# RWKV-7 scan in one backbone layer: one score product per head over four PSUM banks, growth on the transposed matrix, and a new order of steps

## What is computed

```
def step(s, inp):
    w_t, k_t, v_t, kk_t, a_t = inp[:5]
    sa = jnp.einsum('bhvk,bhk->bhv', s, kk_t)
    s = (s * w_t[:, :, None, :] - sa[..., None] * (kk_t * a_t)[:, :, None, :]
         + v_t[..., None] * k_t[:, :, None, :])
    if not want_out:
        return s, None
    return s, jnp.einsum('bhvk,bhk->bhv', s, inp[5])
```

## Time and profile before

| | |
|---|---|
| median of 3 runs | 2215.66 us (2215.59 to 2217.02) |
| the profiled execution | 2217.15 us, of which its span is 2215.5 us |
| busy TensorE, VectorE, ScalarE | 2059.9, 1346.1, 811.3 us |
| mean granted TensorE clock | 0.963 of full |
| the scan | from about 971 us to 1256 us of the span |

### The profile page before, as it was taken

One profiled execution on the slowest core, in us unless ns is written; L12 is line 12 of the kernel. 1 busy time (PEld: TensorE's weight loads), 2 busy tenths in 40 slices (PEclk: granted clock), 3 DMA queues, 4 the chain that ended last, 5 costly groups with the idle time before them and its releaser, 6 DMA issues. The chain is left out here.

```text
span 2215.5 us, 37507 instructions
## 1 busy us (share of the span) xinstructions
PE 2059.9 (93%) x16171; PEld 1695.2 (77%) x16171; DVE 1346.1 (61%) x1258; ACT 811.3 (37%) x890; POOL 278.1 (13%) x135
## 2 busy tenths in 40 slices
PE   7679999999899989977889899979999999999998
PEld 3258888888678876656788788868888888888886
DVE  3465666665628637767888577365665656554444
ACT  1232212123063225625555455354343434333333
POOL 0242213123103305401000020000000000000000
PEclk9589999999989999989999899999999999999999
DMA  9988898987173449996544377535555555555553
GB/s 328 349 284 324 308 322 287 325 309 220 48 219 86 108 139 270 313 236 174 108 89 84 53 223 272 200 123 190 187 188 186 188 188 189 189 193 200 196 189 114
DMA packets 406658, 454.09 MB, mean 205 GB/s; under 512 B 108062, under 2 KB 357262, under 8 KB 389246
## 3 DMA queue, kind: packets, MB, share of 16 engines
q1 hardware_dynamic: 398912, 441.04, 62.9%
q10 hardware_dynamic: 7614, 11.10, 1.4%
HBM read 413.89 MB, written 38.22 MB: 204 GB/s over the span
## 5 line engine op out<-in xcount | busy, mean ns | idle before, releaser
L215 DVE TENSOR_TENSOR f_w_lo<-t_w_raw,f_w_hi 128x2048 fp32r<-128x2048 f32 x132 | 302.3, 2290 | 306.8 <-ACT f_w_hi L209 306.8
L270 PE MATMUL pf<-h,f_w_hi 128*128 128x512 f32 x1320 | 463.9, 395 | 0.0
L209 ACT ACTIVATE f_w_hi<-t_w_raw 128x2048 fp32r<-128x2048 f32 x132 | 253.2, 1918 | 445.6 <-PE pf L270 283.6
L269 PE MATMUL pf<-h,f_w_lo 128*128 128x256 f32 x1320 | 367.4, 278 | 0.3 <-DVE h L2666 0.3
L270 PEld LDWEIGHTS pf<-h,f_w_hi 128*128 128x128 f32 x1320 | 247.6, 188 | 54.3
L269 PEld LDWEIGHTS pf<-h,f_w_lo 128*128 128x128 f32 x1320 | 248.3, 188 | 4.6 <-DVE h L2666 0.6
L209 ACT ACTIVATE p_w_hi<-h_w_raw 128x2048 fp32r<-128x2048 f32 (+1 forms) x52 | 96.4, 1901 | 340.4 <-DVE stage L726 252.1
L261 PE MATMUL p_in<-h,p_w_lo 128*128 128x512 f32 (+1 forms) x512 | 199.3, 389 | 0.0
L259 PE MATMUL p_in<-h,p_w_hi 128*128 128x512 f32 (+1 forms) x512 | 199.3, 389 | 0.0
L260 PE MATMUL p_in<-h,p_w_hi 128*128 128x512 f32 (+1 forms) x512 | 199.2, 389 | 0.0
L858 DVE SCALAR_TENSOR_TENSOR late_acc<-h_of_x,siluc,late_acc 128x2048 f32<-128x2048 f32 x60 | 160.9, 2682 | 38.0 <-DMA h_of_x<-in_ada_w 36.5
(11 more groups left out here) (408 smaller groups left out, 3352.8 us busy)
## 6 DMA issues: line engine op xcount, KB each, us to landing
h_of_x<-in_ada_w SPq DMA_DIRECT2D x64, 1024.0 KB, 5.0
h_w_raw<-in_w_in SPq DMA_DIRECT2D x51, 1024.0 KB, 7.4
t_w_raw<-in_ffn_w_gate SPq DMA_DIRECT2D x44, 1024.0 KB, 5.1
t_w_raw<-in_ffn_w_up SPq DMA_DIRECT2D x44, 1024.0 KB, 5.1
t_w_raw<-in_ffn_w_down SPq DMA_DIRECT2D x44, 1024.0 KB, 4.9
h_w_raw<-in_ada_w SPq DMA_DIRECT2D x32, 1024.0 KB, 8.8
gate_w<-in_w_in SPq DMA_DIRECT2D x32, 1024.0 KB, 6.1
t_w_raw<-in_w_out SPq DMA_DIRECT2D x16, 1024.0 KB, 5.9
```

The costliest lines, as they stand in the source:

```text
L209: act.activation(self.hi[:, m % self.S, 0:w], self.raw[:, s, 0:w], ACT.Copy)\
L215: eng.tensor_tensor(self.lo[:, m % self.S, 0:w], self.raw[:, s, 0:w], b32(self.hi[:, m % self.S, 0:w]), ALU.subtract)\
L269: pe.matmul(hi, wl, x[:, 0, k, :], start=False, stop=False)
L270: return pe.matmul(both, wh, x[:, :, k, :], start=False, stop=last)
```

## The change

`pa` and `pb` become two halves of one tile `pab` of four banks. `scores1` is now the only product of scores. For a latent half chunk the stationary operand is both sources of a head (128 columns) and the moving one both queries (128 columns), so that all four blocks of scores of a head come from one product; for a context half chunk only the query kk moves (64 columns). `first` is twice as wide and holds what `first` and `t2` held. `scores2`, `scores3` on TensorE, `scores2` on VectorE and `t2` are gone. Because the sources are stationary now, the matrix arrives transposed; growth goes on with it transposed (masks of the other direction, operands of `inverse` swapped). The transpose in `open_` is two instructions of 64 partitions each. Every `run_...` list is in another order; `prepare` of VectorE and the exponential after it stand one turn of the loop earlier.

```
-        first = pair_of("first", [U8, C])
+        first = pair_of("first", [2 * U8, C])
-        t2 = pair_of("t2", [U8, C])
-        pa = [psum(st, f"pa{d}", 2 * U8 * C) for d in range(2)]
-        pb = [psum(st, f"pb{d}", 2 * U8 * C) for d in range(2)]
+        pab = [psum(st, f"pab{d}", 4 * U8 * C) for d in range(2)]
+        pa = [p[:, 0:2 * U8 * C] for p in pab]
+        pb = [p[:, 2 * U8 * C:4 * U8 * C] for p in pab]
+        def scored(c, d, q):
+            if not latent(c):
+                return whole(pb[d])
+            return pab[d][:].rearrange("p (n q c) -> p n q c", q=2, c=C)[:, :, q, :]
...
                 def turn(c, d, l, src):
-                    dve.transpose(turned[d][:], src).then_inc(sm("turned", d), 1)
+                    for rows, at in src:
+                        dve.transpose(quads(turned[d][:])[rows], at).then_inc(sm("turned", d), 1)
...
                 def scores1(c, d):
...
-                    dve.copy_predicated(quads(first[d][:]), mask(LOWER, d).bitcast(mybir.dt.uint32), narrow(pb[d]))\
+                    dve.copy_predicated(first[d][:], every_head(STRICT, d).bitcast(mybir.dt.uint32), scored(c, d, 0))\
                        .then_inc(sm("first", d), 1)
-
-                def scores2(c, d):
-                    dve.wait_ge(sm("t2s", d), c + 1)
-                    dve.tensor_tensor(quads(t2[d][:]), narrow(pa[d]), mask(STRICT, d), ALU.mult).then_inc(sm("t2", d), 1)
...
+                    if latent(c):
+                        pe.wait_ge(sm("q2", d), c - 3)
                         pe.wait_ge(sm("S", d), c)
                     for j, h in UNITS:
-                        last = pe.matmul(by_other(pa[d], j, h), source(s12[d], j, h, 1), feat(q12[d][:, :, 0, :], j, h),
-                                         start=True, stop=True)
-                    last.then_inc(sm("t2s", d), 1)
...
+                        sources = s12[d][HEAD[h], j].rearrange("p a c -> p (a c)")
+                        if latent(c):
+                            at = block_of(j, h) * 2 * C
+                            last = pe.matmul(pab[d][:, at:at + 2 * C], sources, q12[d][HEAD[h], j].rearrange("p q c -> p (q c)"),
+                                             start=True, stop=True)
+                        else:
+                            last = pe.matmul(by_block(pb[d], j, h), sources, feat(q12[d][:, :, 0, :], j, h), start=True, stop=True)
...
                 def run_vector(step):
...
-                        every("prepare", 0)
...
+                        every("open", 1)
+                        every("prepare1", 0)
+                        context("stage", 1, 1)
+                        latents("prepare2", 0)
+                        latents("stage", 1, 1)
+                        context("prepare2", 0)
+                        context("stage", 1, 2)
+                        every("prepare", -1)
+                        latents("stage", 1, 2)
```

More of the change, by code:

```diff
@@ L1411, in _ @@
                     dve.tensor_copy(eyes_r[HEAD[h]], own.unsqueeze(1).broadcast_to([C, U8 // 2, C])).then_inc(sm("init", 0), 1)
-                    for t in cross + first:
+                    for t in cross:
                         dve.tensor_copy(t[HEAD[h]], own.unsqueeze(1).broadcast_to([C, U8, C])).then_inc(sm("init", 0), 1)
@@ L1417, in _ @@
                     dve.memset(e2[d][:, :, edge:edge + 1], math.exp(REF)).then_inc(sm("init", 0), 1)
+                dve.wait_ge(sm("cleared", 0), 2)
+                for t in first:
+                    for h in range(2):
+                        own = eye[HEAD[h], HEAD[h]]
+                        dve.tensor_copy(own_blocks(t, h)[HEAD[h]].rearrange("p h u c -> p u h c"),
+                                        own.unsqueeze(1).unsqueeze(1).broadcast_to([C, U8 // 2, 2, C])).then_inc(sm("init", 0), 1)
                 dve.wait_ge(sm("init", 0), 17)
-                dve.wait_ge(sm("cleared", 0), 2)
+                dve.wait_ge(sm("cleared", 0), 4)
                 def prepare(c, d):
@@ L1459, in stage @@
                     dve.wait_ge(sm("level", d), c * GROW + l)
-                    turn(c, d, l, narrow(level(d, l - 1)))
+                    turn(c, d, l, [(slice(0, P), narrow(level(d, l - 1)))])
                 def scores1(c, d):
@@ L1494, in open_ @@
                         dve.wait_ge(sm("step", d), c * GROW)
-                    turn(c, d, 0, first[d][:])
+                    turn(c, d, 0, [(HEAD[b], own_blocks(first[d], b)[HEAD[b]]) for b in range(2)])
                 def state(c, d):
@@ L1637, in _ @@
             def _(pool):
-                for t in S:
+                for t in first + S:
                     pool.memset(t[:], 0.0).then_inc(sm("cleared", 0), 1)
@@ L1649, in _ @@
                 pe.wait_ge(sm("init", 0), 17)
-                pe.wait_ge(sm("cleared", 0), 2)
+                pe.wait_ge(sm("cleared", 0), 4)
                 FOURS = [[(j, 0), (j + 1, 1), (j, 1), (j + 1, 0)] for j in range(0, U8, 2)]
@@ L1718, in flips @@
                 def flips(c, d):
-                    pe.wait_ge(sm("t2", d), c + 1)
+                    pe.wait_ge(sm("first", d), c + 1)
+                    if latent(c):
+                        pe.wait_ge(sm("r12", d), c - 3)
+                    elif c:
+                        pe.wait_ge(sm("S", d), c)
                     for j in range(U8):
@@ L1733, in grow @@
                         pe.wait_ge(sm("vt", d), 2 * c + 2)
-                    src, of = (grown, held(l - 1)) if l else (first, tok)
+                    of = held(l - 1) if l else tok
                     for j, h in UNITS:
-                        last = pe.matmul(placed(l)(level(d, l), j, h), of(step[d], j, h), of(src[d], j, h),
+                        grows = of(grown[d], j, h) if l else first[d][HEAD[j % 2], block_of(j, h), :]
+                        last = pe.matmul(placed(l)(level(d, l), j, h), of(step[d], j, h), grows,
                                          start=True, stop=True)
@@ L1747, in inverse @@
                     for j, h in UNITS:
-                        last = pe.matmul(placed(GROW)(pa[d], j, h), of(grown[d], j, h), of(cross[d], j, h),
+                        last = pe.matmul(placed(GROW)(pa[d], j, h), of(cross[d], j, h), of(grown[d], j, h),
                                          start=False, stop=True, skip_group_check=True)
@@ L1752, in own_part @@
                 def own_part(c, d):
-                    pe.wait_ge(sm("t2", d), c + 1)
+                    pe.wait_ge(sm("first", d), c + 1)
                     pe.wait_ge(sm("vt", d), 2 * c + 2)
                     for j, h in UNITS:
-                        last = pe.matmul(by_token(pb[d], j, h), other(t2[d], j, h), uv[d][HEAD[1 - j % 2], block_of(j, h), :],
+                        last = pe.matmul(by_token(pb[d], j, h), first[d][HEAD[1 - j % 2], block_of(j, h), :], uv[d][HEAD[1 - j % 2], block_of(j, h), :],
                                          start=j < 2, stop=False, skip_group_check=True)
```

125 lines of the change are left out of this document (45 added, 80 removed).

## The result

| | before | after |
|---|---|---|
| median of the runs side by side | 2215.66 us (5 runs, 2211.61 to 2218.58) | 2228.69 us (5 runs, 2224.84 to 2232.94) |
| the profiled execution | 2217.15 us, span 2215.5 | 2224.84 us, span 2223.2 |
| busy TensorE, VectorE, ScalarE | 2059.9, 1346.1, 811.3 us | 2054.6, 1357.4, 810.9 us |
| mean granted TensorE clock | 0.963 | 0.963 |

The ratio is 1.0061, interval 1.0040 to 1.0081. A second series gave 2226.18 against 2214.11, 1.0049 (1.0031 to 1.0067). The forecast was 2216 with a range up to 2226.

The account below looks back on a forecast made before the run. VectorE's own work was taken to set the context period, with TensorE's instruction-fetch pauses lengthening most periods. Context +4.0, latent -2.6 and end -1.0 made +0.4 us: 2216 us on the median, range 2206 to 2226.

Parts of the forecast that it names:

- `first` is now cleared by GpSimd at the start, beside TensorE's gate products: 0: Start of the scan: clearing `first` on GpSimd was to cost 0 us.
- start-up stays: Start of the scan: its share of the 13.2 us excess in context periods was to remain unchanged.
- +4.0: Context half chunks: eight periods were to cost +9.0 us, less 5.0 of pauses given back.
- +0.53: VectorE, every half chunk: wider copy +0.50, two transposes +0.62, one masking of 0.59 gone; +0.53 us of work.
- +0.6: Context half chunks: +0.5 us waiting for the score product, +0.1 for the last growth level and `close`.
- 16.8: Latent half chunks: average period after the change, in us, against 17.17 before; -2.6 us over seven.
- I keep 0.3 of the 1.07 us: Latent periods: of 1.07 us of TensorE pauses per period, 0.3 was to remain.
- -1.0: End of the scan: last copy into `first` to the end of `open_` was to take 5.5 us instead of 6.5.
- The 22.9 stay: End of the scan: the 22.9 us from the end of `open_` to the last sum were to stay unchanged.
- DMA, 0: Loads: VectorE's wait for `ld` behind the prefetch was to be covered by TensorE's pause; 0 us, bounds 0 to 4.
- The rule of the drain: Context score product: by the skill, each of two tiling-mode changes costs some 0.2 us, 1 to 2 in all; not followed.
- The slower rival: Whole scan: pauses stay, VectorE's longer work and its product wait come in full; +10.8 us, 2226 us, chance 0.23.

Follow-up runs that it names:

- split_context: Changed kernel with `first` cleared by ScalarE and the context product written as two of 64x64 per head, output half innermost: 2227.28 us (1.0035).
- split_context_3: Changed kernel, `first` cleared by ScalarE, context product as 64x64 products rotating through all four quarters of the array: 2226.53 us (1.0050).
- split_all_3: Changed kernel, `first` cleared by ScalarE, context and latent products as 64x64 products rotating through the four quarters of the array: 2223.96 us (1.0043).
- after_again: The changed kernel once more, unaltered, beside the kernel before: 2226.18 against 2214.11 us.
- light_vector: Changed kernel, `first` cleared by ScalarE, without half of VectorE's copy into `first` and three quarters of its second transpose: 2218.38 against 2216.68 us.
- before_clears: Kernel before, with GpSimd also clearing two 128x1024 tiles at the start of the scan, ahead of the state: 2215.97 against 2217.98 us.
- clear_on_scalar: Changed kernel with the wide `first` cleared by ScalarE instead of GpSimd: 2225.71 against 2214.11 us (1.0057).
- old_in_new_order: Products, `first`, `t2` and growth of the kernel before, with steps in the changed kernel's order: 2228.11 us (1.0063).
- split_context_2: Changed kernel, `first` cleared by ScalarE, context product as 64x64 products in two groups, upper output rows then lower: 2230.32 us (1.0049).
- split_all: Changed kernel, `first` cleared by ScalarE, context and latent products as 64x64 products in two groups by output half: 2234.48 us (1.0068).
- spread_prefetch: Changed kernel, `first` cleared by ScalarE, the four prefetched weight tiles issued one each in four half chunks: 2229.88 us (1.0050).
- quiet_before: Kernel before, with the weight prefetch behind the last loads and GpSimd's GLA output copy and subtraction moved to VectorE's last wait: 2216.79 us (1.0007).
- quiet_after: Changed kernel, `first` cleared by ScalarE, weight prefetch behind the last loads, GpSimd's GLA output steps moved to VectorE's last wait: 2227.30 us (1.0045).

## Why the prediction was wrong

The forecast was +0.4 us. By the five pieces of the table it was 0, +1.1, +2.9 (seven times 1.13, less 5.0), -2.6 and -1.0, against +3.9, +3.6, +4.4, +3.0 and -2.8. Two steps failed: the start, by 6.4 us, and the latent periods, by 5.6.

**"`first` is now cleared by GpSimd at the start, beside TensorE's gate products: 0", and "start-up stays".** This step failed: +3.9 to the first copy and +3.6 in the first period, of which only 1.1 was forecast. I had looked at who runs beside GpSimd on TensorE and not on VectorE, whose copies are held up beside GpSimd's fillings (1.72 us against 0.41, 0.82 against 0.40) and stand ahead of the first preparation. Two things had to meet: VectorE 1.7 us later than with ScalarE's clearing, and a first product in the 2.00 us form that ran at half clock. ScalarE's clearing gives back 5 of the 7.5 us in the profiles; the longer product and the longer period of every half chunk keep the rest.

**Context, "+4.0" for eight periods.** The mechanism was right, the size nearly. "+0.53" of work is 0.65 (13.39 busy against 12.74: the copy 1.31 instead of 1.22, the transposes 1.44). Wait and close, "+0.6", came as 0.47 for the product and 0.1 more for growth (0.29 against 0.19). Undisturbed periods rose by 1.3, times seven 9.1, and 4.7 of it came back from fewer pauses, where I had given back 5; that leaves +4.4 where +2.9 was forecast. `split_context`, `split_context_3` and `split_all_3` confirm the share of the product.

**Latent, "16.8".** This step failed too, by 5.1 us over seven periods (122.7 against 117.6; the other 0.5 is in the mean of before, 119.7 and not 120.2). "2.0" for the product of 128 moving columns was right (2.06), and the three waits came at 0.60, 0.29 and 0.59 against 0.5, 0.25 and 0.7. Three sizes were off: the stall-free period is 16.7 and not 16.5 (+1.4 in seven); my template, the half chunk of the earlier trace rows, has no sum of outputs, which two periods have (+1.1); and the pauses "I keep 0.3 of the 1.07 us" came out at 0.7 a period (+2.6; seven periods less five of 16.7 and two of 17.3 leave 4.7). Not all of that is pauses: the first latent period of after is 17.86 us, 16.36 where nothing disturbs it (`after_again`), and holds a stretch of half clock from 1129.8 to 1133.2, in which the product took 3.27 us. The pauses themselves did fall as forecast and more (next part). The mistake was to take all of the 1.07 as theirs to give: VectorE's longer work, which `light_vector` shows to be the bound there, fills what they leave.

**The end, "-1.0".** -2.8. `open_` took 5.5 us as worked out. "The 22.9 stay" did not hold, for two reasons. One is the clock: in the last 16 us before, TensorE was granted 0.70 and 0.66 of it, and two of its last groups took 1.97 and 1.74 us; after, it was granted 0.84 and 0.90 and they took 1.15 and 1.13. Before and after:

```profile
1248.00:1256.00 8.00, 6.22 (x156) 5.81 (x150) 0.69 (x1) 2.38 (x4) 0.00 (x0) 0.66 0.01 2
...
1252.00:1258.00 6.00, 3.18 (x98) 2.88 (x98) 3.06 (x6) 1.79 (x3) 0.00 (x0) 0.84 0.00 0
1258.00:1265.30 7.30, 5.25 (x162) 4.67 (x161) 0.69 (x1) 2.33 (x4) 0.00 (x0) 0.90 0.02 4
```

From the start of the last level of growth (1244.03 before, 1255.20 after) to the end that is 11.9 us against 10.1. In `split_context_3`, which has the changed lists and a clock as low as before there, it is 11.8, so these 1.8 us are the clock and not the change's work; why the clock fell less was not tried. The other reason is ahead of that level, where the clock is full: from the end of `open_` to it are 11.0 us before and 9.9 after, 1.1 us less in the changed kernel, which the prediction had left as they were. With the 1.0 of `open_` the three make the 3.9 us between these two profiles; between the means it is 2.8.

**DMA, 0.** Nearly right, but "`prepare` one turn earlier" is only the loop's numbering: on VectorE `prepare` stands behind the second level of growth in both lists (1071.44 before, 1079.80 after, each behind `q_f`). `ld` is late behind the prefetch by 1.08 us (2.44 in `after_again`), within the bounds, and TensorE's pause, which had covered that, is gone.

**The rule of the drain.** It was rightly set aside. The full-height product starts 0.63 us after the 64x64 growth ahead of it (1082.92, 1083.55), the 64x64 one in `split_context_3` 0.52 (1060.98, 1061.50): a change of shape costs 0.11 us. The Trainium skill (TensorEngine Tiling, Key Properties) speaks of a drain; no wait longer than this shows here.

**The rivals.** The slower rival had 2226 and a chance of 0.23; that its number was near is luck. It let the pauses stay, and in context they went nearly wholly, which the prediction had named as a sign that it was wrong. The time came from the start and from the latent half chunks, whose sizes no rival had.

## Were the pauses waits for instructions?

Yes. Let a pause be over 0.4 us between two multiplications of one group. From 1000 to 1240 us the traces of before, `before_clears`, after, `after_again`, `clear_on_scalar`, `split_context_3` and `old_in_new_order` have some 80 of them, and all stand at a multiple of 256 of TensorE's recorded instructions (within 8 of it, some records being missing). One piece of the instruction queue, 16 KB, is loaded for each 256, and the engine goes on 1.1 to 1.75 us after the piece has landed. The dose follows, with all pauses of this kind, those between two groups too, from the start of one multiplication to the start of the next, in seven context and seven latent periods. The instructions include waits, and records that are missing are filled in:

| | instructions per context half chunk | pauses, us | per latent | pauses, us |
|---|---|---|---|---|
| before, `before_clears` | 819, 816 | 11.2, 8.8 | 1012 | 11.5, 11.5 |
| `old_in_new_order` | 817 | 12.6 | 1010 | 3.8 |
| the changed products as they are (8 traces) | 752 | 0.0 to 3.5 | 883 | 3.2 to 6.8 |
| `split_context`, `_2`, `_3` | 806 to 816 | 9.4, 9.6, 11.7 | 883 | 3.2 to 4.1 |
| `split_all_3` | 814 | 10.4 | 947 | 7.2 |

The 64 instructions that the change takes out of a context half chunk take 8 us of pauses with them, and 64 put back in another way bring them back. In the latent half chunks the number alone doesn't decide: `old_in_new_order` has the many instructions and few pauses, its waits for other engines are longer. And the 15 us of pauses that are gone gave back 4.7 us in context and at most 2.8 in latent (seven times 1.07, less the 4.7 that are left), since a pause counts only where VectorE has nothing left to do.

## What to carry to other kernels

Cost an initialization at every engine that it can hold up, here VectorE beside GpSimd, and follow it to the first product: here a slow product that came late, after 2.32 us of idle time, ran at half clock. Where two engines hand work to and fro, take a stall-free period of each kind with all its optional steps, and count of a pause only the part that the other engine leaves idle. Fewer and larger products save instructions, but a product of 64 rows and 128 columns took 2.00 us where two of 64x64 took 1.11, and it needs an order of steps of its own. Before you read the price of a sequence from one group, look at the clock granted in it: at half clock 1.11 us became 1.99.

## What the runs showed of the hardware

- Four recorded multiplications of 64x64, which are two products of the code, start within 58 ns if the two write different halves of the output partitions, in all sequences tried (before; `split_context`, `split_context_3`, 1.11 us for 64 of them), and about every 117 ns if all of a group write the same half (`split_context_2`, 1.87 us). Of 64 rows and 128 columns two start every 112 ns, whether 64 or 128 columns move. With 128 moving columns four of 64x64 need 109 ns (`split_all_3`, 1.98 us), and 218 ns if they write the same half (`split_all`, 3.3 us). All these are at full clock; at half clock four of the first kind need 106 ns (`split_context`, 1.99 us).
- VectorE's instruction beside a GpSimd subtraction of 128x2048 lasted 2.67, 4.79 and 5.54 us instead of 0.69 to 1.22, in `after`, `before_clears` and `spread_prefetch`, by where it fell; in before one lasted 1.35 instead of 0.69, and in `after_again` none was stretched.
- While 4 MB of prefetch are in the queues, the next piece of instructions is late: idle times of 4.51 us (before), 2.79 (`before_clears`), 2.84 (`quiet_before`) and 1.97 (`quiet_after`), in other places of the scan.
